# Product 3's rounding and low half behind softplus and key copies, and quarter projections by token half

## The reference

```python
xn = rmsnorm(x, norm_gain)
rq, rk, rv, rg, sq, sk, sv, sg, gr, gs = split(xn @ w_in)     # 2048 x 14336
# stick-breaking attention, 8 heads of 128, each token against the earlier ones (samples: 512 cached keys too)
z = q . k / sqrt(128) + bias_h
log_keep = where(mask, log_sigmoid(-z), 0)
after = reverse_cumsum(log_keep) - log_keep
a = where(mask, exp(log_sigmoid(z) + after), 0);  o_sb = a @ v
# retention, 8 heads, per-head decay, rotary on q and k, chunks of 128, a state per sequence
merged = sigmoid(gr) * ((GN(o_ret) * silu(rg)) @ w_ret_proj) + sigmoid(gs) * ((o_sb * silu(sg)) @ w_sb_proj)
y = rmsnorm(x + merged @ w_out) * final_norm_gain
```

## Time and profile before

| | us |
|---|---|
| median of 3 runs (2047.74 to 2048.61) | 2048.49 |
| the profiled execution's own time | 2047.92 |
| its span | 2045.7 |
| PE busy | 2007.0 (98%) |
| DVE busy | 1537.7 (75%) |
| ACT busy | 997.8 (49%) |
| POOL busy | 113.0 (6%) |

### The profile page before, as it was taken

One profiled execution on the slowest core, in us unless ns is written; L12 is line 12 of the kernel. 1 busy time (PEld: TensorE's weight loads), 2 busy tenths in 40 slices (PEclk: granted clock), 3 DMA queues, 4 the chain that ended last, 5 costly groups with the idle time before them and its releaser, 6 DMA issues.

```text
span 2045.7 us, 42383 instructions
## 1 busy us (share of the span) xinstructions
PE 2007.0 (98%) x15572; PEld 1951.3 (95%) x15572; DVE 1537.7 (75%) x2053; ACT 997.8 (49%) x1458; POOL 113.0 (6%) x133
## 2 busy tenths in 40 slices
PE   7999999999999999999999999999999999999996
PEld 6999999999999999999999999999999999999996
DVE  6877767777683277888888888888887855468786
ACT  5546555465554245454555545554554632234443
POOL 0022210222200000000000000000000000000000
PEclk8999999999999999999999999999999999999998
DMA  4445555455554434434344333433446354544444
GB/s 156 135 134 144 149 147 155 139 141 148 148 174 135 149 112 133 121 84 128 110 117 127 112 118 112 119 116 115 131 138 209 119 173 151 172 152 111 121 120 143
DMA packets 456803, 277.23 MB, mean 136 GB/s; under 512 B 20739, under 2 KB 436867, under 8 KB 455555
## 3 DMA queue, kind: packets, MB, share of 16 engines
q1 hardware_dynamic: 454532, 271.22, 44.9%
q10 hardware_dynamic: 2176, 4.72, 0.6%
HBM read 235.76 MB, written 40.11 MB: 135 GB/s over the span
## 4 chain that ended last, share of the span: by engine, by line
PE 92%; DVE 2%; ACT 2%; DMA 1%; issue 1%; DVEq 1%; ACTq 0%; SPq 0%
PE ACC L827 42%; PE ACC L833 21%; PE ACC L733 16%; PE Z L753 4%; PE Z L973 1%; PE Z L952 1%; PE Z L863 1%; PE ACC L1280 1%; DMA scratch_gate_r<-RG 1%; PE ACC L779 1%; PE Z L1053 1%; ACT LL L1402 0%; PE Z L879 0%; ACT LL L1400 0%; DVE TTL L2448 0%
## 5 line engine op out<-in xcount | busy, mean ns | idle before, releaser
L1357 ACT ACTIVATE HI_B<-RAW 128x1024 fp32r<-128x1024 f32 x186 | 197.2, 1060 | 440.5 <-DVEq L1927 253.9
L1903 DVE TENSOR_TENSOR LO_B<-RAW,HI_B 128x1024 fp32r<-128x1024 f32 x186 | 227.6, 1224 | 88.8 <-ACT HI_B L1357 73.8
L827 PE MATMUL ACC<-TH,HI_C 128*128 128x288 f32 x864 | 235.6, 299 | 0.0
L827 PE MATMUL ACC<-XH,HI_A 128*128 128x288 f32 x864 | 235.0, 299 | 0.5 <-ACT HI_A L1357 0.5
L827 PE MATMUL ACC<-XH,HI_B 128*128 128x288 f32 x864 | 234.0, 297 | 0.0
L827 PE MATMUL ACC<-TL,HI_C 128*128 128x288 f32 x864 | 231.2, 295 | 0.0
L827 PE MATMUL ACC<-XL,HI_B 128*128 128x288 f32 x864 | 231.1, 295 | 0.0
L827 PE MATMUL ACC<-XL,HI_A 128*128 128x288 f32 x864 | 230.9, 294 | 0.0
L1903 DVE TENSOR_TENSOR LO_A<-RAW,HI_A 128x1024 fp32r<-128x1024 f32 x124 | 154.0, 1242 | 33.1 <-ACT HI_A L1357 22.4
L827 PEld LDWEIGHTS ACC<-XH,HI_A 128*128 128x128 f32 x864 | 162.2, 188 | 15.2 <-issue 9.1
L1903 DVE TENSOR_TENSOR LO_C<-RAW,HI_C 128x1024 fp32r<-128x1024 f32 x124 | 156.7, 1264 | 15.0 <-issue 7.4
(11 more groups left out here) (442 smaller groups left out, 4729.9 us busy)
## 6 DMA issues: line engine op xcount, KB each, us to landing
RAW<-in_w_in SPq DMA_DIRECT2D x224, 512.0 KB, 3.9
RAW<-in_w_out SPq DMA_DIRECT2D x33, 512.0 KB, 4.5
KV<-in_cache_sb_k SPq DMA_DIRECT2D x256, 64.0 KB, 1.9
KV<-in_cache_sb_v SPq DMA_DIRECT2D x256, 64.0 KB, 1.9
RAW<-in_w_ret_proj SPq DMA_DIRECT2D x32, 512.0 KB, 4.1
RAW<-in_w_sb_proj SPq DMA_DIRECT2D x16, 512.0 KB, 4.0
ST<-in_state_ret SPq DMA_DIRECT2D x64, 128.0 KB, 2.9
out<-ST SPq DMA_DIRECT2D x64, 128.0 KB, 2.0
```

Source lines behind the costliest of these rows:

```text
L827: mm = pe.matmul(to, weight(HI, HI_EO, w, k), x[:, k, :], start=at == 0 and x is xh, stop=False)
L1357: act.activation(block_of_slot(HI, HI_C4, SLOT[pos]), by_parity(RAW[:, SRC[n]], SLOT[pos]), ACT.Copy).then_inc(S["hi_made"], 1)
L1903: dve.tensor_tensor(block_of_slot(LO, LO_C4, SLOT[pos]), by_parity(RAW[:, SRC[n]], SLOT[pos]), block_of_slot(HI, HI_C4, SLOT[pos]).bitcast ...
```

## The change

In a stick-breaking head's first pair (u = 0, all eight heads) `third_last` is set. ScalarE then issues `hi(3)` after `softplus` and `even_keys(0)` instead of ahead of the copy of product 0, and VectorE issues `lo(3)` after the three `log_keep` (in `sb_attention(3)`) instead of ahead of the first combination. In `quarter` the loop over token halves becomes the outermost: twelve matmuls of half 0, then twelve of half 1. No instruction is added or taken away.

```diff
--- before.py
+++ after.py
@@ -727,9 +727,9 @@
                 if first:
                     t.room(f"acc_read{a}")
                 t.take(f"w_full{s}")
-                for k in range(QK):
-                    for w, x in ((HI, xh), (HI, xl), (LO, xh)):
-                        for half in range(2):
+                for half in range(2):
+                    for k in range(QK):
+                        for w, x in ((HI, xh), (HI, xl), (LO, xh)):
                             mm = pe.matmul(ACC[a][:, half, 0:HALF], w[s // 2][:, s % 2 * QK + k, :],
                                            x[:, k0 + k, half * HALF:(half + 1) * HALF],
                                            start=first and k == 0 and w is HI and x is xh,
@@ -1357,16 +1357,18 @@
                 act.activation(block_of_slot(HI, HI_C4, SLOT[pos]), by_parity(RAW[:, SRC[n]], SLOT[pos]), ACT.Copy).then_inc(S["hi_made"], 1)
 
 
-            def pair(dst, ready, after, first=False, made=0):
+            def pair(dst, ready, after, first=False, made=0, third_last=False):
 
                 for n in range(7):
-                    if n >= made:
+                    if n >= made and not (third_last and n == 3):
                         hi(n, first)
                     if n == 3:
                         ready()
                         t.past("prod", 1)
                         act.activation(dst[:, 0, 0:HALF], BANK[0], ACT.Copy).then_inc(S["p1_copied"], 1)
                     after(n)
+                    if third_last and n == 3:
+                        hi(n, first)
                 t.skip("prod", 7)
                 t.skip("sum_made", 4)
                 t.skip("comb", 7)
@@ -1517,7 +1519,7 @@
                             act.activation(GS_T[:, :, :], GS_T[:, :, :], ACT.Ln, bias=1.0).then_inc(S["ln_made"], 1)
                         if not new and u == 1 and n == 6:
                             sigmoid(QK_)
-                    pair(dst, nothing, after, first and u == 0, 1 if first and u == 0 else 0)
+                    pair(dst, nothing, after, first and u == 0, 1 if first and u == 0 else 0, u == 0)
 
             for q in range(16):
                 if q == 3:
@@ -1927,7 +1929,7 @@
                 dve.drain().then_inc(S["sum_made"], 1)
                 dve.tensor_tensor(RAW[:, 2], RAW[:, 4], RAW[:, 2], ALU.add).then_inc(S["sum_made"], 1)
 
-            def pair(dst, last, after, made=0):
+            def pair(dst, last, after, made=0, third_last=False):
 
                 if made == 0:
                     lo(0)
@@ -1943,7 +1945,7 @@
                 t.take("a12_in", 16)
                 dve.tensor_tensor(RAW[:, 4], RAW[:, 1], RAW[:, 4], ALU.subtract).then_inc(S["sum_made"], 1)
                 after(2)
-                if made < 4:
+                if made < 4 and not third_last:
                     lo(3)
                 t.take("p1_copied")
                 t.past("prod", 2)
@@ -2028,6 +2030,7 @@
                     odd_keys(1)
                     for o, m in SEG[::-1]:
                         log_keep(o, o + m)
+                    lo(3)
                     new_values()
                     odd_keys(3)
                 if n == 5:
@@ -2096,7 +2099,7 @@
                                 .then_inc(S["qk_low"], 1)
                         if not new and u == 1:
                             gate_parts(n - 1, QK_, GS_T)
-                    pair(dst, None if first and u == 0 else (VG, QK_)[u], after, 1 if first and u == 0 else 0)
+                    pair(dst, None if first and u == 0 else (VG, QK_)[u], after, 1 if first and u == 0 else 0, u == 0)
 
             for q in range(16):
                 if q < 12:
```

## The result

The changed kernel runs in 2036.26 us (median of 4 runs, 2035.55 to 2038.63), the kernel before in 2048.55 (4 runs, 2047.74 to 2049.02). The ratio is 0.9942, with a 95% interval of 0.9926 to 0.9957: faster by 12.3 us, 0.6%. The forecast was 2035.6. The profiled execution took 2036.05 with a span of 2033.8, 11.9 less than before.

A forecast was written before the change was run, and what follows sets the result against it. TensorE, busy 98%, was taken to bound the kernel through matmul distances and its waits. 9.9 (heads) + 3.0 (quarters) = 12.9 off 2047.92 gives 2035.0, as a median 2035.6 us; range 2033.8 to 2040.6.

The forecast's parts named there:

- The wait and what made it: In each of 8 heads TensorE waits for ScalarE's copy of keys, queued behind softplus and a waiting rounding; 9.9 us.
- part one: In 8 stick-breaking heads, moving product 3's rounding and low half back in their queues removes TensorE's wait; 9.9 us gained.
- Up: the whole 9.9 us, the list's entry: Upper bound of the gain in the heads: the full wait for L1408 in TensorE's list, 9.9 us.
- SP's later load of a11: SP's load waits for lo(3) and goes out at 291.9; first reader at 303.28, over 11 us later, cost nothing.
- Rival 2: Half the head's wait comes back at group_logits(0), VectorE having lo(3) and new values ahead of odd_keys(3); 2039.6 us, 12%.
- the cover of `odd_keys(3)`: In each head, keys copied by VectorE at 293.7 to 294.3, read by TensorE at 295.10; 0.8 to 1.4 us spare.
- Rival 4: In the heads, lo(3) is held until GpSimd's masks and sums end, product 3 waits 2.45; slower, 2055.5 us, 4%.
- Part two: In the quarter stages, ordering matmuls by token half avoids alternating banks; 131.7 ns a matmul, 3.0 us gained.
- So I put 1.1 to 1.4 ns on the alternation: In the quarters, two banks taken in turn were held to cost 1.1 to 1.4 ns a matmul.
- Two comparisons: Same-bank places, Strassen products at 131.8 ns and first_tile at 131.6, against 132.8 to 133.1 in the quarters.
- rival 1: Order of halves in quarter changes nothing; the 133 ns come from something else, for instance x slices; 2038.6 us, 11%.
- The upper bound of this part: Most the quarters' new order could gain: 3.7 us, with 131.6 ns throughout and nothing given back.

The follow-up runs named there:

- e1_heads_only: The changed kernel without the new order of token halves in the quarters, only product 3's rounding and low half moved; median 2037.94 us, ratio 0.9947 to the kernel before.
- e4_alt_banks: The changed kernel with each quarter matmul going to the other of two PSUM banks than the one before it; median 2037.17 us, ratio 0.9943 to the kernel before.
- e7 to e11: Five kernels: the changed kernel with all SBUF tensors, or those behind RAW, XL or XH, 32 bytes up, or behind RAW 64; medians 2035.85 to 2047.97 us.

## Why the prediction was right, and where it was not

**The wait and what made it: right.** The chain by which ScalarE's rounding held up the softplus and the copy of keys went as read. Moved by the 4.60 us: copy of product 0 at 284.57 (forecast 284.6), softplus 284.88 (284.9), copy of keys 288.74 (288.8), rounding 289.22 (289.25), low half 290.52 to 291.82 (290.55 to 291.8), copy of keys 3 done at 293.74 (293.7). SP's later load of a11 hurt nothing: no wait for a rounding has come into the heads.

**The size of part one: too small.** The step that failed is "Up: the whole 9.9 us, the list's entry". The head is 1.43 shorter for a wait of 1.20. The trace of before has the low half of product 2 ahead of the earlier trace rows's `cached(2)` so:

```profile
289.70 1.21 PE L833 MATMUL ACC<-TH,LO_C 128*128 128x288 f32 x8
```

From the start of product 2's low half to `cached(2)` it was 2.41 before (289.70 to 292.11) and is 1.05 now, which is 1.36. The idle time in the list is counted from the shown end of the last matmul, and that lies 0.16 after the point where the next one could have started: a matmul is shown with 0.29 us where the distance of two starts is 0.13. Another 0.06 is the slow first transpose after the wait. Part one gave 11.7 for the 9.9 (six times 1.43, and more in the first and last head, whose waits were longer), and e1_heads_only alone measured the same 11.7.

**The late rivals: rightly small.** Rival 2 named the next wait: 1.34 us of delay bring it up (0.2 at L863), so the cover of `odd_keys(3)` is just over 1 us, as worked out (0.8 to 1.4). Rival 4's block did not come: the low half took 1.30 beside GpSimd, and it was GpSimd's sum that waited, 1.25 where it had taken 0.46 before:

```profile
293.63 0.46 POOL L2603 TENSOR_TENSOR LL<-LL 128x128 f32<-128x128 f32 x1
```

That agrees with a block by one instruction, as the Trainium skill, SBUF — State Buffer, "SBUF: two separate sides", has it, and it fell on the engine with time to spare.

**Part two: wrong.** The step was "So I put 1.1 to 1.4 ns on the alternation". It gave 0.4 us in w_sb, 0.1 in w_ret and nothing measurable as a whole, for 3.0 forecast. Two comparisons, with the products and with `first_tile`, spoke for the bank, but both differed from the quarters in more than that. e4_alt_banks took the bank alone and found nothing; e7 to e11 took addresses alone and moved the mean of the gate_s pairs by up to 1.6 ns, so a gap of 1.2 ns can come from where the operands lie. That it does come from there in the quarters is not shown. In the first projections the changed `quarter` reads half 1 from the same addresses and in the same order within a slot as `first_tile` does, and inside the last three slots its trace has 132.4 ns a matmul against 131.2 all the same. Addresses alone do not explain that, and its cause stays open. The outcome was rival 1's, which had 11% and the x slices as a possible cause. The Trainium skill's advice to use all banks (Perfetto Trace Analysis, Matmul Optimizations) neither gained nor lost here, where two banks were taken in turn or one after the other: 101.85 against 101.84 us. The upper bound of this part was also added up wrong: with 131.6 throughout, its three terms come to 3.4, not 3.7.

The total was right within 0.7 us by luck: 1.8 too little in part one stood beside some 2.9 too much in part two, which gave 0.1 net in the changed kernel's trace. With the measured parts the forecast would have been 2048.5 - 11.7 - 0.1 = 2036.7.

## What to carry to other kernels

When the busiest engine waits for a copy that stands in another engine's queue, look for an instruction ahead of it there that is itself waiting, and move that one behind, with everything that hangs on it on a third engine: here the rounding moved without its low half was worth nothing. Count such a wait from start to start, not by the idle time shown. A difference of one per cent between two places of matmuls is no evidence for a mechanism until one thing alone has been changed; and a tensor put in or taken out below others may do as much as a whole change to the schedule, as 64 bytes did here.

## What the runs showed of the hardware

- In the gate_s pairs the distance of two matmuls (128x128 weights, 288 columns, fp32r) ranges over 127 to 138 ns by position and is the same in every pair, and in every run with this layout, to about 0.5 ns. Its mean went from 131.8 to 133.4 ns when the weights and all behind them were put 64 bytes further from x, and did not change when everything was shifted by 32 bytes.
- The order of the same matmuls alone made a difference in w_sb: 133.1 ns in the old order and 132.6 in the new, both with the banks taken in turn (before and e4_alt_banks).
- Consecutive matmuls into one PSUM bank or into two in turn: the same to 0.01 us in 768 (101.84 and 101.85).
- A VectorE subtraction with two SBUF inputs took 1.30 us beside GpSimd's work instead of 1.23, and a GpSimd addition next to it 1.25 instead of 0.46.
- A wait of TensorE shown as 1.20 us of idle time made a head 1.43 longer.
